# Output projection in a fused layer: weights fetched as pairs of 512 KB, side loads moved, two pairs of products at the step's head

## The reference, cut to what matters

```
branches = [(ya, a_z), (yb, b_z), (yc, c_z), (yd, d_z), (ym, m_z)]
mixed = jnp.concatenate([y.astype(x.dtype) * jax.nn.silu(z) for y, z in branches], axis=-1)
return x + mixed @ w_out        # mixed: 2048 x 1280, w_out: 1280 x 1024
```

## Time and profile before

| | |
|---|---|
| time, three runs | 5008.44 us median (5006.63 to 5010.34) |
| the profiled execution | 5015.02 us, span 5013.4 us |
| TensorE matmul busy | 4250.0 us, 85% of the span |
| VectorE, ScalarE, GpSimd busy | 53%, 39%, 15% |
| mean granted TensorE clock | 0.857 |
| step k = 2 begins | 1380 us |
| step k = 15 ends | 2489 us |
| weight slices fetched in all | 600 of 256 KB, 3.2 us to landing |

### The profile page before, as it was taken

One profiled execution on the slowest core, in us unless ns is written; L12 is line 12 of the kernel. 1 busy time (PEld: TensorE's weight loads), 2 busy tenths in 40 slices (PEclk: granted clock), 3 DMA queues, 4 the chain that ended last, 5 costly groups with the idle time before them and its releaser, 6 DMA issues. The chain is left out here.

```text
span 5013.4 us, 66174 instructions
## 1 busy us (share of the span) xinstructions
PE 4250.0 (85%) x23522; PEld 3149.5 (63%) x23522; DVE 2656.4 (53%) x5590; ACT 1937.1 (39%) x4022; POOL 732.9 (15%) x755
## 2 busy tenths in 40 slices
PE   7997899985788899989879999977788887877589
PEld 5885777775566666666658888833344444555467
DVE  3113444444566655555411111068889888888546
ACT  3112232323333333333311101034677767767621
POOL 3111111100100000000000000022223333434500
PEclk9998999986588888989889999966578887787789
DMA  5326656664465555454352211210000001010033
GB/s 187 123 108 218 221 201 226 199 214 148 143 215 198 194 172 177 158 173 154 113 183 90 82 66 69 59 60 19 19 20 20 20 20 38 20 39 18 32 136 116
DMA packets 293737, 585.32 MB, mean 117 GB/s; under 512 B 47944, under 2 KB 80364, under 8 KB 293244
## 3 DMA queue, kind: packets, MB, share of 16 engines
q1 hardware_dynamic: 293408, 581.10, 34.1%
HBM read 453.03 MB, written 127.94 MB: 116 GB/s over the span
## 5 line engine op out<-in xcount | busy, mean ns | idle before, releaser
L3051 PE MATMUL ds_big<-ds_ikT,ds_iqT 64*128 64x512 f32 (+3 forms) x608 | 385.2, 767 | 76.3 <-ACT ds_iqT L3028 56.4
L3518 POOL TENSOR_TENSOR ds_E<-ds_bT 128x256 f32<-128x256 f32 x112 | 72.1, 643 | 2410.9 <-ACT ds_bT L3487 2232.1
L301 PE MATMUL g_acc<-g_ws_hi,g_hT_hi 128*128 128x512 f32 (+1 forms) x1024 | 386.9, 378 | 0.0
L302 PE MATMUL g_acc<-g_ws_lo,g_hT_hi 128*128 128x512 f32 (+1 forms) x1024 | 385.3, 376 | 0.0
L303 PE MATMUL g_acc<-g_ws_hi,g_hT_lo 128*128 128x512 f32 (+1 forms) x1024 | 385.2, 376 | 0.0
L529 PE MATMUL mm_big<-mm_gw_hi,mm_ghT_hi 128*128 128x512 f32 (+1 forms) x768 | 322.0, 419 | 30.9 <-PEq L134 30.9
L3107 DVE TENSOR_SCALAR_CACHE_REDUCE ds_seen<-ds_eq,ds_num 128x2048 uint16<-128x2048 uint16 (+13 forms) x224 | 331.3, 1479 | 26.3 <-issue 4.3
L531 PE MATMUL mm_big<-mm_gw_hi,mm_ghT_lo 128*128 128x512 f32 (+1 forms) x768 | 303.2, 395 | 0.0
L530 PE MATMUL mm_big<-mm_gw_lo,mm_ghT_hi 128*128 128x512 f32 (+1 forms) x768 | 302.7, 394 | 0.0
L3147 ACT ACTIVATE ds_signs<-ds_lo,ds_at 128x2048 bf16<-128x2048 uint16 (+13 forms) x224 | 291.3, 1301 | 2.1 <-issue 0.7
L328 DVE COPY g_stage<-g_acc 128x512 f32<-128x512 f32 (+1 forms) x64 | 41.5, 649 | 459.2 <-PE g_acc L303 459.2
(11 more groups left out here) (550 smaller groups left out, 10117.7 us busy)
## 6 DMA issues: line engine op xcount, KB each, us to landing
fox_ow<-halves SPq DMA_DIRECT2D x600, 256.0 KB, 3.2
mm_ghT_hi<-turned SPq DMA_DIRECT2D x96, 512.0 KB, 4.0
mm_ghT_lo<-turned SPq DMA_DIRECT2D x96, 512.0 KB, 5.1
proj<-g_stage SPq DMA_DIRECT2D x112, 256.0 KB, 2.0
proj<-mm_gstage SPq DMA_DIRECT2D x80, 256.0 KB, 5.0
mm_x<-proj SPq DMA_DIRECT2D x64, 256.0 KB, 3.7
second_raw<-in_w_in SPq DMA_DIRECT2D x56, 256.0 KB, 4.0
proj<-fp_stage SPq DMA_DIRECT2D x48, 256.0 KB, 2.0
```

The lines of the kernel that those rows point to most:

```text
L301: pe.matmul(sums, hT.hi[:, k, tile], wt.hi[:, k, 0:width], start=(k == 0), stop=False)
L302: pe.matmul(sums, hT.hi[:, k, tile], wt.lo[:, k, 0:width], start=False, stop=False)
L3051: pe.matmul(big[:, n % 2, 0:wd], iqT[o, h // 2], b.ikT[o, x:x + wd], start=True, stop=True)\
```

## The change

The output projection's weights are fetched as pairs: one transfer of 512 KB brings the hi and the lo slice of one block and half, 20 transfers a step, into two double slots (`OUT_PAIRS = 2`; the fifth slot of `ow` is left unused in these steps). Pair q's transfer waits until pair q-2 was used; `o_used` now counts once a pair, after the third matmul, and all three matmuls of a pair wait for the whole pair. Two pairs are fetched ahead for the next step.

In the steps with weights ahead the places of the first half's blocks change: blocks 0 and 1 stand at 0.0 and 0.0002, so that their six matmuls open the step on TensorE, and blocks 2 to 9 stand from 0.06 to 0.34, 0.04 apart. The second half and step 2 keep their places.

The side loads on SyncE move: the three loads of `mixed` from place 0.04 to 0.44 (not in step 1), the load of `z` from 0.02 to 0.5, the RWKV loads from 0.15 to 0.55. The store of the previous result goes from the step's beginning to just before pair 5's transfer (0.104), the load of `x` to just before pair 7's (0.184). `out_last_two` keeps its 40 transfers and five slots.

```diff
+OUT_PAIRS = 2
...
-        yield 0.75 if split else 0.04
+        yield 0.75 if split else 0.44
...
-    arrived = (s.ow_in0, s.ow_in1, s.ow_in2, s.ow_in3, s.ow_in4)
-    slices = [(n, j, a) for n in range(2) for j in range(OUT_K) for a in range(2)]
+    arrived = (s.ow_in0, s.ow_in1)
+    pairs = [(n, j) for n in range(2) for j in range(OUT_K)]
     halves = x[:].rearrange("p (n c) -> p n c", n=2)
-    at = lambda n, j: 0.005 + 0.4 * n + 0.37 * j / OUT_K
+    def at(n, j, a=0):
+
+        if n == 0 and j < 2 and ahead:
+            return 0.0002 * j
+        if n == 0 and ahead:
+            return 0.06 + 0.32 * (j - 2 + 0.4 * a) / (OUT_K - 2)
+        return 0.005 + 0.4 * n + 0.37 * (j + 0.4 * a) / OUT_K
 
     def sync(sp):
         yield 0.0
         if not ahead:
-            for q in range(OUT_SLOTS):
+            for q in range(OUT_PAIRS):
                 weights(sp, q, arrived[q])
-        if t:
-            sp.dma_start(b.x_out[(t - 1) * P:t * P, :], x[:]).then_inc(s.ox_stored, 16)
-        for q in range(OUT_SLOTS, len(slices)):
-            n, j, a = slices[q - OUT_SLOTS]
-            yield at(n, j + 0.5 * a + 0.5)
-            if q == 2 * OUT_SLOTS:
+        for q in range(OUT_PAIRS, len(pairs)):
+            n, j = pairs[q - OUT_PAIRS]
+            yield at(n, j) + 0.004
+            if q == OUT_K // 2 and t:
+                sp.dma_start(b.x_out[(t - 1) * P:t * P, :], x[:]).then_inc(s.ox_stored, 16)
+            if q == OUT_K // 2 + 2:
                 if t:
                     sp.wait_ge(s.ox_stored, 16)
                 sp.dma_start(x[:], b.x_old[tok, :]).then_inc(s.ox_in, 16)
 
-            sp.wait_ge(s.o_used, q - OUT_SLOTS + 1)
-            weights(sp, q, arrived[q % OUT_SLOTS])
+            sp.wait_ge(s.o_used, q - OUT_PAIRS + 1)
+            weights(sp, q, arrived[q % OUT_PAIRS])
...
     def weights(sp, q, signal):
-        n, j, a = slices[q]
-        sp.dma_start(wr[:, q % OUT_SLOTS].bitcast(F32), b.split_d[OUT_ROWS[j], a, :, cols(n)]).then_inc(signal, 16)
+        n, j = pairs[q]
+        sp.dma_start(wr[:, 2 * (q % OUT_PAIRS):2 * (q % OUT_PAIRS) + 2].bitcast(F32),
+                     b.split_d[OUT_ROWS[j], :, :, cols(n)].rearrange("a p c -> p a c")).then_inc(signal, 16)
...
                 landed(pe, q)
-                whi, wlo = wr[:, q % OUT_SLOTS], wr[:, (q + 1) % OUT_SLOTS]
+                whi, wlo = wr[:, 2 * (q % OUT_PAIRS)], wr[:, 2 * (q % OUT_PAIRS) + 1]
                 pe.matmul(bank, mS.hi[:, j], whi, start=(j == 0), stop=False)
-                pe.matmul(bank, mS.lo[:, j], whi, start=False, stop=False).then_inc(s.o_used, 1)
-                landed(pe, q + 1)
+                pe.matmul(bank, mS.lo[:, j], whi, start=False, stop=False)
                 pe.matmul(bank, mS.hi[:, j], wlo, start=False, stop=(j == OUT_K - 1)).then_inc(s.o_used, 1)
...
         if k + 1 < TILES:
-            yield 0.02
+            yield 0.5
             sp.dma_start(b.z[:, (k + 1) % 2], proj[(k + 1) * P + PAD:(k + 2) * P + PAD, B_Z:B_Z + GW])\
...
         if i + 1 < TILES:
-            yield 0.15
+            yield 0.55
             n = rwkv_loads(B, sp, s.r_ahead, proj, i + 1, s.shifted)
```

More of the change, by code:

```diff
@@ L1384, in sync @@
                 sp.dma_start(x[:], b.x_old[tok, :]).then_inc(s.ox_in, 16)
-            sp.wait_ge(s.o_used, q - OUT_SLOTS + 1)
-            weights(sp, q, arrived[q % OUT_SLOTS])
+            sp.wait_ge(s.o_used, q - OUT_PAIRS + 1)
+            weights(sp, q, arrived[q % OUT_PAIRS])
         yield at(1, OUT_K) + 0.02
         if t + 3 < TILES:
-            sp.wait_ge(s.o_used, len(slices))
-            for q in range(OUT_SLOTS):
+            sp.wait_ge(s.o_used, len(pairs))
+            for q in range(OUT_PAIRS):
                 weights(sp, q, s.ow_ahead)
             yield 1.0
-            sp.wait_ge(s.ow_ahead, 16 * OUT_SLOTS)
+            sp.wait_ge(s.ow_ahead, 16 * OUT_PAIRS)
     def weights(sp, q, signal):
-        n, j, a = slices[q]
-        sp.dma_start(wr[:, q % OUT_SLOTS].bitcast(F32), b.split_d[OUT_ROWS[j], a, :, cols(n)]).then_inc(signal, 16)
+        n, j = pairs[q]
+        sp.dma_start(wr[:, 2 * (q % OUT_PAIRS):2 * (q % OUT_PAIRS) + 2].bitcast(F32),
+                     b.split_d[OUT_ROWS[j], :, :, cols(n)].rearrange("a p c -> p a c")).then_inc(signal, 16)
     def landed(pe, q):
         if not ahead:
-            pe.wait_ge(arrived[q % OUT_SLOTS], 16 * (q // OUT_SLOTS + 1))
-        elif q >= OUT_SLOTS:
-            pe.wait_ge(arrived[q % OUT_SLOTS], 16 * (q // OUT_SLOTS))
+            pe.wait_ge(arrived[q % OUT_PAIRS], 16 * (q // OUT_PAIRS + 1))
+        elif q >= OUT_PAIRS:
+            pe.wait_ge(arrived[q % OUT_PAIRS], 16 * (q // OUT_PAIRS))
     def tensor(pe):
@@ L1409, in tensor @@
             for j in range(OUT_K):
-                q = (n * OUT_K + j) * 2
+                q = n * OUT_K + j
                 yield at(n, j)
@@ L1424, in vector @@
             yield at(n, OUT_K) + 0.01
-            dve.wait_ge(s.o_used, 2 * OUT_K * (n + 1))
+            dve.wait_ge(s.o_used, OUT_K * (n + 1))
             if n == 0:
```

## The result

The changed kernel takes 5037.57 us (median of 7, 5025.17 to 5060.20), the kernel before 5008.44 us (7 runs, 4997.96 to 5020.15). The ratio is 1.0063, 95% interval 1.0042 to 1.0085: slower by 0.6%, 29 us by the medians. I had forecast 4990 us, faster by 18, in a range of 4960 to 5032.

The account below looks back on a forecast made before the run. TensorE's own time (work, clock, waits) was taken to bound the kernel. Opening -34, double slots with side loads +15 and k = 2 +1 gave -18 us, so 4990 us from a median of 5008.4; range 4960 to 5032.

Parts of the forecast that it names:

- What bounds the kernel: Steps k = 3 to 15: TensorE, busy 90%, sets a step by its work, clock and waits; no other engine passes 57%.
- Part 1: Six products at the step's head: the clock rises earlier, gain 34 us, bounds 0 and 55 us.
- Part 2: Twenty 512 KB transfers into two double slots: waits of 25 us in thirteen steps, today's 10.0 us go, net 15 us lost.
- 7 us on average: Head of each step: time at the low clock before it rises, against 12.8 us today; bounds 4.4 and 12.8 us.
- The price of a low microsecond: Heads of the steps: each microsecond at the low clock costs 0.45 us; direct bound 0.5.
- rival C: Two slots are too few, waits 60 us, clock's gain halved: +34, 5042 us, slower; chance 0.22.
- Part 3: Side loads moved to mid-step: the head's queue empties, today's 10.0 us of waits go; some tenths of wait behind RWKV loads.
- Part 4: Step k = 2, no weights ahead: first products wait for 512 KB instead of 256 KB, 1 us lost.
- B: Rival: the clock does not care, gains 0 to 10 us that waits take back; 5008 us, within a few; chance 0.18.

## Why the prediction was wrong

The steps k = 3 to 15 of four profiles split the change. Idle is the length less TensorE's busy time. By the scatter seen above, differences of some 15 us between two such rows can be chance; the ratios are timed.

| us | length | busy | idle | ratio, timed |
|---|---|---|---|---|
| before | 1037.6 | 931.8 | 105.8 | 1 |
| + side loads | 1032.6 | 932.2 | 100.4 | 0.9977 |
| + two double slots | 1091.5 | 959.8 | 131.7 | 1.0104 |
| + opening (the change) | 1073.9 | 933.3 | 140.6 | 1.0063 |

*What bounds the kernel.* Right: TensorE's clock and its waits account for the added time. VectorE's and ScalarE's busy times did not move.

Two steps failed, one in Part 1 and one in Part 2; the one in Part 2 turned the sign.

*Part 1, the opening: -34 us forecast, -18 measured (-26.5 busy, +8.9 idle).* This is its worth inside the double slots; with five slots it is worth nothing that can be told (0.9972 against 0.9977, and 1.0011 alone). The clock does rise at the end of the six products, in 12 of 13 heads and at the time forecast. The step that failed here is "7 us on average": I counted only the first stretch at the low clock and took it that the clock, once up, stays. It falls again at 10 to 14 us, for 116 us in the thirteen steps together. The idle time that it adds is pair 5's wait. The price of a low microsecond was right: from the third to the fourth row of the table the time at the low clock falls from 306 to 256 us and busy time by 26.5 us, 0.52 each.

*Part 2, the double slots, +15 us net: the step that failed and turned the sign.* Measured are 58.9 us between the second and the third row (31.3 idle, 27.6 busy), 64 by the ratios. Two things in its working were wrong.

First, the waits in the changed kernel: 25 us forecast, 57.4 measured. By position they are 3.2 us at pairs 2 and 3, 14.0 at pair 4 (I had 18), 18.2 at pair 5 (I had "a few tenths"), and 22.0 from pair 12 on (tenths again), all of these in the seven shorter steps up to k = 9. The median landing was right (4.2 us forecast and measured), but not the use of one landing for all: pair 5's transfer, which SyncE issues just behind the 512 KB store of x, lands in 5.3 us, and the pair behind the RWKV loads, pair 16, in 6.2. The store itself lands in 5.3 us after 2.9. And an average distance of 5.2 to 5.7 us against 4.4 hid the pairs closer together. The 14.0 and most of the 22.0 us belong to the double slots: without the opening they are 16.6 and 20.4, with five slots in the new order 0 and 9.0. Pair 5's belong to the new places, which put it right behind pair 4 (2.8 us without the opening, 18.4 with five slots, 0.5 with pair 5 at its old place), and to what stands ahead of it in the queue; moving the store of x alone was not run.

Second, a price put at nothing: I counted each wait once, as idle time, and gave the loss through the clock to rival C only. Busy time rises by 27.6 us, and the timed clocks fall as well (0.860 to 0.854); smaller and earlier transfers gave 27.6 us of busy time back.

*Part 3, the side loads: right in sign,* about -5 us in the profiles and -0.23% timed. I had written that all of today's 10.0 us of waits go; with five slots 8.0 stay, 5.4 of them still in the head. With double slots no gain of the move can be told (1.0094 without it, 1.0104 with it). The Trainium skill's rule, from "DMA: Bandwidth & Descriptors", section "Queues, rings and completion order", that an engine takes descriptors in ring order, fits what the later RWKV loads did to the pair behind them (2.6 us of waits to none).

*Part 4, k = 2:* 1 us forecast, 6.5 measured. Waits for weights there go from 7.8 to 13.5 us.

*The rivals.* C was the right one, at 0.22, with 5042 us against 5037.6, and in part by luck. Its condition ("from a landing of about 5 us on") was wrong: at a median of 4.2 us it holds already. Its waits were right, 36 us in the five short steps (35.1 measured) and 24 in the others (22.3). So were its uneven places, and its halved gain of the opening (17, measured 18), but that is against the kernel without the opening: against the kernel before, the clock gave nothing, 931.8 to 933.3 us of busy time. B's sign, a mean clock of 0.68 to 0.72 in the heads, came true as well, 0.72, because the second fall took the gain of the first rise. The Trainium skill's fit of 3.2 us for 512 KB ("DMA: Bandwidth & Descriptors", "Anatomy of one DMA — SWDGE (gpsimd) path"), an estimate for another path, was to be set aside: the rows showed 4.2.

Not settled: what the second fall hangs on. Taking most of the waits away (a quarter of each transfer) and bringing the RWKV chain forward both came with fewer falls, 5 of 13 steps each in one profile, the second a lucky one, and neither removed it; moving pairs 5 to 9 did not help. No kernel with three pairs was run.

## What to carry to other kernels

Size a prefetch by its closest consumers, not by the average distance: list for each transfer the end of the use that frees its slot and the start of the use that needs it, with the clock at its high level, and every one below the landing is a wait. Take the landing at that place in the queue, not the median: behind another 512 KB it was a microsecond longer. One more small buffer was worth more here (five single slots against four: 34 us) than anything that the pairing changed at four. And where TensorE's clock moves, price a wait twice, as idle time and as slower work behind it; and follow the clock through the whole step, since it can fall again behind the work pulled forward to raise it, as in 12 of 13 steps here. For this kernel the best found in full is the new order with the five single slots kept (0.9972), hardly apart from moving the side loads alone (0.9977).

## What the runs showed of the hardware

The clock stayed at the low level while TensorE was busy almost without a gap, in four heads of the kernel before for 18 us (busy 19.8 to 19.9 us of 20): there narrow matmuls, and those over 65 or 16 rows, stood between the products. In the changed kernel, with six wide ones in a row at the head, it rose within 4.7 us in 12 of 13 heads, and in the same order with five slots within 5.0 us in 10. Transfers of 512 KB in rows of 2 KB, at most two pairs in flight, landed in 4.2 us as a median, but in 5.3 us right behind the 512 KB store and in 6.2 us behind the two RWKV loads; those of 128 KB in rows of 512 B in 2.3 us, of 256 KB in 3.1 to 3.7 us.
